# Four of eight gate/up K-steps as three single-pass products, one buffer for the down parts, and a new order on ScalarE and VectorE

## The chip, the core and the metric

One core of a Trainium2 chip. The metric is the device time of one execution in microseconds (us), the median of several. TensorE does matrix products and transposes, ScalarE (ACT) copies and activations, VectorE (DVE) elementwise work, GpSimd (POOL) here issues the indexed gathers and scatters, SyncE (SP) issues the plain loads and stores. The engines run side by side and wait for each other on semaphores.

## The reference, cut to what matters

A diffusion backbone step over 256 context and 1024 latent tokens (1280 rows of 1024). A mixing layer is followed by a mixture of 16 experts, of which each token takes two; both carry float32 data.

```python
gate = jnp.einsum('btd,edf->btef', h, w_eg)      # d = 1024, f = 256, 16 experts
up = jnp.einsum('btd,edf->btef', h, w_eu)
a = jax.nn.silu(gate) * up * combine.astype(h.dtype)[..., None]   # combine: 2 experts of 16 per token
return jnp.einsum('btef,efd->btd', a, w_ed)
```

The result, scaled by a gate row, is added to the residual, and a last RMS norm follows. The change touches the expert part only.

## The kernel before, in words

The kernel first runs the modulation, projection, Fourier, convolution and mLSTM parts, then the output projection and router (to about 800 us of the span). The router's result sorts the 2560 (token, expert) pairs by expert into slots of 128 rows; each slot has one expert. The inputs give 27 slots, numbered 0 to 26 here. All numbers of slots, the expert of a slot (`eidI`), the place of its weights (`offI`) and each expert's last slot (`endI`) are read from tables at run time by register loads.

*Weights.* An expert takes `WE` = 6144 columns of float32 in each of 128 partitions: 4096 for gate and up (8 K-steps of 512 columns) and 2048 for down. Three experts fit in `wexp`, a ring. SP loads an expert in three pieces of 1 MB (line 645). The load of expert e + 3 waits until the last slot of expert e has been through `down` (`dn_ps`, line 663), and until all earlier loads have landed (`w_full`).

*One slot.* POOL gathers its 128 rows of `h2` from memory into `xg` (`fetch`, line 772). TensorE transposes them (`x_trans`, line 1580) into two PSUM banks; ScalarE copies them out (`x_chan`, lines 1137 and 1138). `gate_up` accumulates 8 K-steps of 128 x 512 in one bank, silu comes from ScalarE (`gate_silu`, line 1166), the product with up from VectorE (`product`, line 2188). `a_trans` (line 1602) transposes the result, `down` multiplies it into 1024 columns (two banks), `out_rows` on VectorE computes the gate row (`gate_rows`, line 2216) and scales the rows (`scaled_rows`, line 2223), and POOL adds them to `acc_scratch` in memory by an indexed scatter (`add_rows`, line 791). A scatter waits for the one before (`added`); the gather for a later slot is behind it in POOL's queue.

*Products in parts.* Most products are plain float32 (two records in the trace for one K-step). Others are split: an operand is copied to a type called fp32r, the high part, and what is left over is a second fp32r operand, the low part. Three single-pass products, high x high, low x high and high x low, then take the place of one float32 product. Before the change `SK` = 2 of the 8 gate/up K-steps and all of down are done in parts. High parts are ScalarE copies (`gate_high` line 1151, `down_high` line 1161, `a_high` line 1142, the second copy of `x_chan`); low parts are VectorE subtractions (`gate_low` line 2203, `down_low` line 2211, `a_low` line 2192, `x_low` line 2197). `esplit` holds the parts of gate/up and down of two slots.

*Order.* TensorE's loop has in step n: `a_trans` of slot n, `x_trans` of slot n + 2, `gate_up` of slot n + 1, `down` of slot n. ScalarE's in step n: `a_high` (n), `x_chan` (n + 2), `down_high` (n + 1), `gate_silu` (n + 1), `gate_high` (n + 2). VectorE's: `a_low` (n), `x_low` (n + 2), `down_low` (n + 1), `product` (n + 1), `out_rows` (n), `gate_low` (n + 2). The orders are written out by hand. `gate_high` and `down_high` load two registers each, then wait for the weights of their slot. In the last steps VectorE also makes two one-hot rows (`slot_owner`, line 2264), since the last two slots' rows are added on TensorE instead of by a scatter; SP loads the sums for the final norm after the second of these. Ahead of the loop VectorE runs `slot_weights` and `slot_weights_in`; the latter waits for products of TensorE (`per_slot`) that come after `gate_up` of slot 0.

## Time and profile before

| | us |
|---|---|
| median of 3 runs | 1139.44 |
| lowest, highest | 1138.89, 1149.29 |
| the profiled execution | 1137.51 |
| its span | 1135.7 |
| TensorE busy in the span | 1045.4 (92%) |
| VectorE busy | 668.5 (59%) |
| ScalarE busy | 417.9 (37%) |

The profiler records one execution. The span runs from its first to its last instruction; all times in rows below are us from its start unless marked ns. In a timeline row stand the start, the time, the engine (PE is TensorE's matmuls, PEld its weight loads, SPq and POOLq the queues that issue DMAs), the line of the kernel, the operation, its output and inputs and how many instructions were merged; in square brackets the idle time of the engine before it and what ended it.

### The profile page before, as it was taken

The page shows a single profiled execution, that of the slowest core. Times are in us where ns is not written, and L with a number is a line of the kernel's source. Part 1 is how long each engine was busy: PE and PEld are TensorE (multiplying, and loading weights), DVE is VectorE, ACT ScalarE, POOL GpSimd, SP SyncE. Part 2 cuts the span into 40 slices and gives each one's busy share as a digit, 9 for nine tenths or more (in the row PEclk, how much of TensorE's full clock was granted, in tenths as well). Part 3 has the DMA queues.
Part 4 walks back from the last instruction along what each step waited for, and adds up shares of the span by engine and source line. Part 5 has one row for each costly group of instructions (what it writes and reads, how often), then busy time and mean ns, then how long its engine had stood idle before and what let it go on. Part 6 is the DMA issues. An engine that isn't in the chain of part 4 may idle for free.

```text
span 1135.7 us, 18439 instructions
## 1 busy us (share of the span) xinstructions
PE 1045.4 (92%) x6090; PEld 789.5 (70%) x6091; DVE 668.5 (59%) x1137; ACT 417.9 (37%) x816; POOL 200.0 (18%) x240
## 2 busy tenths in 40 slices
PE   6899999999999999989877999992699999989997
PEld 3899999989999986569764444541456666656665
DVE  3445885177798410119994443366666666666677
ACT  3443223244322246246662111121244445444444
POOL 2010000000000002002355000000233433333413
PEclk9899999999999998999998999996799999999999
DMA  9934333314342231322136222225748889887957
GB/s 370 343 126 147 118 140 131 111 57 148 111 142 102 94 135 47 93 87 64 54 50 241 111 90 97 93 93 203 278 124 276 274 250 280 268 301 228 320 147 291
DMA packets 59303, 188.36 MB, mean 166 GB/s; under 512 B 8018, under 2 KB 20818, under 8 KB 53106
## 3 DMA queue, kind: packets, MB, share of 16 engines
q1 hardware_dynamic: 49924, 154.81, 38.0%
q0 software_dynamic: 7632, 27.79, 10.2%
q10 hardware_dynamic: 1696, 5.10, 1.1%
q8 instruction: 29, 0.48, 0.2%
q14 instruction: 22, 0.18, 0.0%
HBM read 153.52 MB, written 34.16 MB: 165 GB/s over the span
## 4 chain that ended last, share of the span: by engine, by line
PE 80%; DVE 9%; DMA 3%; issue 2%; ACT 2%; POOL 1%; SPq 1%; POOLq 0%; ACTq 0%; DVEq 0%
PE psum L1345 43%; PE psum L1287 29%; DVE RW L1922 3%; PE psum L1580 2%; DVE RE L1949 1%; PE psum L1211 1%; DMA RB<-in_w_exp 1%; DMA RA<-in_w_ada 1%; DVE RE L1957 1%; PE psum L1500 1%; PE psum L1302 1%; DMA RW<-h_scratch,idxc 1%; PE psum L1227 1%; PE psum L1266 1%; PE psum L1602 0%
## 5 line engine op out<-in xcount | busy, mean ns | idle before, releaser
L1287 PE MATMUL psum<-input_parts,weight_parts 128*128 128x320 f32 x2208 | 339.3, 313 | 1.7 <-DVE input_parts L1721 1.7
L1287 PEld LDWEIGHTS psum<-input_parts,weight_parts 128*128 128x128 f32 x2208 | 325.7, 189 | 10.4 <-issue 6.9
L1345 PE MATMUL psum<-RB,RW 128*128 x324 | 148.0, 607 | 6.1 <-DMA RB<-in_w_exp 3.5
L921 ACT ACTIVATE weight_parts<-RW 128x1024 fp32r<-128x1024 f32 x46 | 48.7, 1058 | 224.7 <-PE psum L1287 224.7
L1345 PE MATMUL psum<-expert_parts 128*128 128x512 f32 x486 | 126.5, 413 | 1.1 <-DVE expert_parts L2192 1.1
L1728 DVE TENSOR_TENSOR weight_parts<-RW,weight_parts 128x1024 fp32r<-128x1024 f32 x46 | 56.3, 1225 | 113.4 <-ACT weight_parts L921 113.2
L1345 PEld LDWEIGHTS psum<-expert_parts 128*128 128x128 f32 x486 | 91.3, 188 | 31.7 <-issue 13.5
L1345 PEld LDWEIGHTS psum<-RB,RW 128*128 128x128 f32 x324 | 60.8, 195 | 74.7 <-issue 74.6
L1345 PE MATMUL psum<-RS,RB 128*128 128x512 f32 (+1 forms) x200 | 80.1, 555 | 1.4 <-DVE RE L1949 1.2
L1345 PE MATMUL psum<-RC,RB 128*128 128x512 f32 x160 | 74.8, 613 | 0.0
L732 POOL TENSOR_TENSOR RE<-RE,RA 2x2304 f32<-2x2304 f32 (+1 forms) x2 | 9.0, 4520 | 348.6 <-DMA RA<-in_b_ada 348.5
L2211 DVE TENSOR_TENSOR expert_parts<-RB,expert_parts 128x1024 fp32r<-128x1024 f32 x54 | 63.7, 1222 | 9.8 <-ACT expert_parts L1161 9.0
L1345 PEld LDWEIGHTS psum<-RS,RB 128*128 128x128 f32 x200 | 37.1, 190 | 38.1 <-issue 35.0
L1740 DVE SCALAR_TENSOR_TENSOR RB<-RB,colv 128x15 f32<-128x15 f32 x120 | 57.3, 552 | 0.0
L1161 ACT ACTIVATE expert_parts<-RB 128x1024 fp32r x54 | 54.1, 1049 | 6.5 <-issue 5.8
L1345 PEld LDWEIGHTS psum<-RC,RB 128*128 128x128 f32 x160 | 30.0, 197 | 31.1 <-issue 31.1
L1151 ACT ACTIVATE expert_parts<-RB 128x1024 fp32r x27 | 28.6, 1061 | 61.4 <-DMA RB<-in_w_exp 38.7
L2223 DVE SCALAR_TENSOR_TENSOR RE<-psum,maskf,RC 128x1024 f32<-128x1024 f32 x27 | 34.6, 1283 | 23.7 <-PE psum L1345 21.8
L2066 DVE TENSOR_TENSOR RA<-psum,RB 128x1024 f32<-128x1024 f32 x10 | 12.2, 1224 | 57.3 <-PE psum L1345 57.1
L791 POOL DMA_INDIRECT acc_scratch<-RE,idxsc x25 | 44.0, 1758 | 7.2 <-issue 7.1
L1166 ACT ACTIVATE RB<-psum 128x256 f32<-128x256 f32 x27 | 10.3, 383 | 92.2 <-PE psum L1345 92.2
L2188 DVE TENSOR_TENSOR RB<-RB,psum 128x256 f32<-128x256 f32 x27 | 11.4, 421 | 54.8 <-ACT RB L1166 54.6
(351 smaller groups left out, 1522.7 us busy)
## 6 DMA issues: line engine op xcount, KB each, us to landing
RB<-in_w_exp SPq DMA_DIRECT2D x48, 1024.0 KB, 8.9
RW<-in_w_in SPq DMA_DIRECT2D x46, 512.0 KB, 4.1
RW<-in_w_ada SPq DMA_DIRECT2D x34, 512.0 KB, 3.3
RA<-in_w_ada SPq DMA_DIRECT2D x10, 512.0 KB, 14.1
RW<-gm_scratch SPq DMA_DIRECT2D x20, 256.0 KB, 3.4
h_scratch<-RE SPq DMA_DIRECT2D x10, 512.0 KB, 2.6
acc_scratch<-RA SPq DMA_DIRECT2D x10, 512.0 KB, 3.6
RB<-acc_scratch SPq DMA_DIRECT2D x10, 512.0 KB, 8.6
```

What stands on the lines that cost most here:

```text
L791: nc.gpsimd.indirect_dma_start(acc_dram, bass.IndirectOffsetOnAxis(ap=idxsc[:, r], axis=0), yb[:, r], None, compute_op=ALU.add).then_inc(a ...
L921: nc.scalar.activation(spl[:, r, 0], raw[:, r], ACT.Copy).then_inc(whi_ok, 1)
L1151: nc.scalar.activation(esplit[:, r, 0, 0:G_U], wexp[:, bass.ds(off, G_U)], ACT.Copy).then_inc(whi_ok, 1)
L1161: nc.scalar.activation(esplit[:, r, 0, G_U + j * D:G_U + (j + 1) * D], wexp[:, bass.ds(off + (D_U + j * D), D)], ACT.Copy)\
L1287: last = nc.tensor.matmul(psum[:, 2 * r + g, 0:GW], spl[:, r, wv, k], hT[:, xv, k, g * GW:(g + 1) * GW], start=(k == 0 and wv == 0 and xv ...
L1345: return nc.tensor.matmul(out, lhsT, rhs, start=start, stop=stop, **kw_)
L1580: last = nc.tensor.transpose(psum[:, 4 + k // 4, (k % 4) * P:(k % 4 + 1) * P], xg[:, r, k * P:(k + 1) * P], ident[:, :])
L1728: nc.vector.tensor_tensor(spl[:, r, 1], raw[:, r], spl[:, r, 0].bitcast(F32), ALU.subtract).then_inc(wlo_ok, 1)
L1740: nc.vector.scalar_tensor_tensor(out, u[:, bass.ds(i, n)], colv[:, bass.ds(i * 2 + (C_WDW + j), 1)], out, ALU.mult, ALU.add).then_inc(conv, 1)
L1922: nc.vector.scalar_tensor_tensor(Dm[:, n % 2, hd], nmb[:, n % 2, hd], gcol[:, 0, t, d, hd:hd + 1], (maskf if d == 0 else maskb)[:, :], ALU ...
L2211: nc.vector.tensor_tensor(esplit[:, r, 1, c], wexp[:, bass.ds(off + (D_U + j * D), D)], esplit[:, r, 0, c], ALU.subtract)\
L2223: nc.vector.scalar_tensor_tensor(yb[:, r].rearrange("p (b c) -> p b c", b=2), psum[:, bank:bank + 2, :], wslot[:, col], gates.rearrange("p ...
```

## The change

`SK` goes from 2 to 4: four gate/up K-steps are float32, four are in parts. The low part of x moves to a place in `RW` that the smaller `xT` frees. `esplit` is replaced by `gsplit` (gate/up parts of two slots, 2048 columns each) and one `dsplit` for the down parts of one slot; the last slot's down parts go to the gate/up buffer `lsplit` that is free by then. `gate_high` and `gate_low` have two instructions each. `down_high` and `down_low` work on slot n in step n, not n + 1. The order becomes, on ScalarE in step n: `a_high` (n), `down_high` (n), `x_chan` (n + 2), `gate_high` (n + 2), `gate_silu` (n + 1); on VectorE: `a_low` (n), `down_low` (n), `x_low` (n + 2), `gate_low` (n + 2), `product` (n + 1), `out_rows` (n). TensorE's order stays.

```diff
-SK = 2
+SK = 4
...
     with nc.sbuf_tensor("expert_parts", [P, 8 * T + 4 * D], F32R) as expert_parts:
-        esplit = expert_parts[:, 0:12 * D].rearrange("p (b v n) -> p b v n", b=2, v=2)
+        gsplit = expert_parts[:, 0:8 * D].rearrange("p (b v n) -> p b v n", b=2, v=2)
+        dsplit = expert_parts[:, 8 * D:12 * D].rearrange("p (v n) -> p v n", v=2)
+        lsplit = gsplit[:, 1]
         aTh, aTl = (expert_parts[:, c:c + 2 * FE].rearrange("p (b j t) -> p b j t", b=2, j=2) for c in (12 * D, 12 * D + 2 * FE))
...
@@ -1148,17 +1153,17 @@
             if read is not None:
                 act.wait_ge(gu_ps, read)
             act.wait_ge(x1_out, 16 * (NT - BATCH))
-            nc.scalar.activation(esplit[:, r, 0, 0:G_U], wexp[:, bass.ds(off, G_U)], ACT.Copy).then_inc(whi_ok, 1)
-
-        def down_high(r, blk, read):
+            for q in range(2):
+                nc.scalar.activation(gsplit[:, r, 0, q * D:(q + 1) * D], wexp[:, bass.ds(off + q * D, D)], ACT.Copy).then_inc(whi_ok, 1)
+
+        def down_high(dst, blk, done, read):
             need = act.value_load(eidI[0:1, blk], min_val=16 * WPART, max_val=16 * WPART * NE)
             off = act.value_load(offI[0:1, blk], min_val=0, max_val=2 * WE)
             act.wait_ge(w_full, need)
-            if read is not None:
-                act.wait_ge(dn_ps, read)
+            act.wait_ge(done, read)
             act.wait_ge(x1_out, 16 * (NT - BATCH))
             for j in range(2):
-                nc.scalar.activation(esplit[:, r, 0, G_U + j * D:G_U + (j + 1) * D], wexp[:, bass.ds(off + (D_U + j * D), D)], ACT.Copy)\
+                nc.scalar.activation(dst[:, 0, j * D:(j + 1) * D], wexp[:, bass.ds(off + (D_U + j * D), D)], ACT.Copy)\
                     .then_inc(whi_ok, 1)
...
         gate_high(0, slice(0, 1), None)
         x_chan(0, 1)
-        down_high(0, slice(0, 1), None)
+        gate_high(1, slice(1, 2), None)
         gate_silu(0, 1)
         x_chan(1, 2)
-        act.wait_ge(tok_ps, 2)
-        gate_high(1, slice(1, 2), None)
+
+        def step(j, n):
+            a_high(j, n + 1)
+            down_high(dsplit, bass.ds(n, 1), dn_ps, n + 1)
+            x_chan(j, n + 3)
+            gate_high(j, bass.ds(n + 2, 1), n + 1)
+            gate_silu(1 - j, n + 2)
+
         with act.Fori(0, pairs) as i:
             for j in range(2):
-                r = 1 - j
-
-                a_high(j, i * 2 + (1 + j))
-                x_chan(j, i * 2 + (3 + j))
-                down_high(r, bass.ds(i * 2 + (1 + j), 1), i * 2 + (1 + j))
-                gate_silu(r, i * 2 + (2 + j))
-                gate_high(j, bass.ds(i * 2 + (2 + j), 1), i * 2 + (1 + j))
+                step(j, i * 2 + j)
+        step(0, pairs * 2)
         n = pairs * 2 + 1
-        a_high(0, n)
-        x_chan(0, n + 2)
-        down_high(1, bass.ds(n, 1), n)
-        gate_silu(1, n + 1)
-        gate_high(0, bass.ds(n + 1, 1), n)
         a_high(1, n + 1)
+        down_high(dsplit, bass.ds(n, 1), dn_ps, n + 1)
         x_chan(1, n + 3)
-        down_high(0, bass.ds(n + 1, 1), n + 1)
+        down_high(lsplit, bass.ds(n + 1, 1), gu_ps, n + 1)
         gate_silu(0, n + 2)
         a_high(0, n + 2)
...
             for k in range(SK, KD):
-                mm(psum[:, r, :], xT[:, r, k], wexp[:, bass.ds(off + k * 2 * FE, 2 * FE)], k == SK, False)
+                mm(psum[:, r, :], xT[:, r, k - SK], wexp[:, bass.ds(off + k * 2 * FE, 2 * FE)], k == SK, False)
             pe.wait_ge(xl_ok, have)
             pe.wait_ge(wlo_ok, split)
             for k in range(SK):
                 for xp, v in ((xTh, 0), (xTl, 0), (xTh, 1)):
-                    last = mm(psum[:, r, :], xp[:, r, k], esplit[:, r, v, k * 2 * FE:(k + 1) * 2 * FE], False,
+                    last = mm(psum[:, r, :], xp[:, r, k], gsplit[:, r, v, k * 2 * FE:(k + 1) * 2 * FE], False,
                               k == SK - 1 and v == 1)
             last.then_inc(gu_ps, 1)
...
-        gate_up(0, slice(0, 1), 1, SPLIT0 + 1)
+        gate_up(0, slice(0, 1), 1, SPLIT0 + 2)
         per_slot(blkw, 3, 3, 4)
         x_trans(1, 16, 1)
         with pe.Fori(0, pairs) as i:
             for j in range(2):
                 a_trans(j, i * 2 + (1 + j))
                 x_trans(j, i * 16 + 32, i * 2 + (2 + j))
-                gate_up(1 - j, bass.ds(i * 2 + (1 + j), 1), i * 2 + (2 + j), i * 6 + (SPLIT0 + 4 + 3 * j))
-                down(j, i * 2 + (1 + j), i * 6 + (SPLIT0 + 3 + 3 * j))
+                gate_up(1 - j, bass.ds(i * 2 + (1 + j), 1), i * 2 + (2 + j), i * 8 + (SPLIT0 + 4 + 4 * j))
+                down(j, i * 2 + (1 + j), i * 8 + (SPLIT0 + 6 + 4 * j), dsplit)
         a_trans(0, pairs * 2 + 1)
-        down(0, pairs * 2 + 1, pairs * 6 + (SPLIT0 + 3), 0)
+        down(0, pairs * 2 + 1, pairs * 8 + (SPLIT0 + 4), lsplit, 0)
...
         def gate_low(r, blk, split):
             off = dve.value_load(offI[0:1, blk], min_val=0, max_val=2 * WE)
-            dve.wait_ge(whi_ok, split)
-            nc.vector.tensor_tensor(esplit[:, r, 1, 0:G_U], wexp[:, bass.ds(off, G_U)], esplit[:, r, 0, 0:G_U], ALU.subtract)\
-                .then_inc(wlo_ok, 1)
-
-        def down_low(r, blk, split):
+            for q in range(2):
+                dve.wait_ge(whi_ok, split + q)
+                c = slice(q * D, (q + 1) * D)
+                nc.vector.tensor_tensor(gsplit[:, r, 1, c], wexp[:, bass.ds(off + q * D, D)], gsplit[:, r, 0, c], ALU.subtract)\
+                    .then_inc(wlo_ok, 1)
+
+        def down_low(dst, blk, split):
             off = dve.value_load(offI[0:1, blk], min_val=0, max_val=2 * WE)
             for j in range(2):
                 dve.wait_ge(whi_ok, split + j)
-                c = slice(G_U + j * D, G_U + (j + 1) * D)
-                nc.vector.tensor_tensor(esplit[:, r, 1, c], wexp[:, bass.ds(off + (D_U + j * D), D)], esplit[:, r, 0, c], ALU.subtract)\
+                c = slice(j * D, (j + 1) * D)
+                nc.vector.tensor_tensor(dst[:, 1, c], wexp[:, bass.ds(off + (D_U + j * D), D)], dst[:, 0, c], ALU.subtract)\
                     .then_inc(wlo_ok, 1)
...
         x_low(0, 1)
         slot_weights()
-        down_low(0, slice(0, 1), SPLIT0 + 2)
         slot_weights_in()
+        gate_low(1, slice(1, 2), SPLIT0 + 3)
         product(0, 1)
         x_low(1, 2)
-        gate_low(1, slice(1, 2), SPLIT0 + 4)
+
+        def step(j, n):
+            at = lambda k: slice(n + k, n + k + 1) if isinstance(n, int) else bass.ds(n + k, 1)
+            a_low(j, n + 1)
+            down_low(dsplit, at(0), n * 4 + (SPLIT0 + 5))
+            x_low(j, n + 3)
+            gate_low(j, at(2), n * 4 + (SPLIT0 + 7))
+            product(1 - j, n + 2)
+            out_rows(j, n, at(0))
+
         for j in range(2):
-            a_low(j, 1 + j)
-            x_low(j, 3 + j)
-            down_low(1 - j, slice(1 + j, 2 + j), SPLIT0 + 5 + 3 * j)
-            product(1 - j, 2 + j)
-            out_rows(j, j, slice(j, j + 1))
-            gate_low(j, slice(2 + j, 3 + j), SPLIT0 + 7 + 3 * j)
+            step(j, j)
         with dve.Fori(0, pairs) as i:
             for j in range(2):
-                a_low(j, i * 2 + (3 + j))
-                x_low(j, i * 2 + (5 + j))
-                down_low(1 - j, bass.ds(i * 2 + (3 + j), 1), i * 6 + (SPLIT0 + 11 + 3 * j))
-                product(1 - j, i * 2 + (4 + j))
-                out_rows(j, i * 2 + (2 + j), bass.ds(i * 2 + (2 + j), 1))
-                gate_low(j, bass.ds(i * 2 + (4 + j), 1), i * 6 + (SPLIT0 + 13 + 3 * j))
+                step(j, i * 2 + (2 + j))
         n = pairs * 2 + 2
-        a_low(0, n + 1)
-        x_low(0, n + 3)
-        down_low(1, bass.ds(n + 1, 1), pairs * 6 + (SPLIT0 + 11))
-        product(1, n + 2)
-        out_rows(0, n, bass.ds(n, 1))
-        gate_low(0, bass.ds(n + 2, 1), pairs * 6 + (SPLIT0 + 13))
+        step(0, n)
         a_low(1, n + 2)
-        down_low(0, bass.ds(n + 2, 1), pairs * 6 + (SPLIT0 + 14))
+        down_low(dsplit, bass.ds(n + 1, 1), pairs * 8 + (SPLIT0 + 17))
+        down_low(lsplit, bass.ds(n + 2, 1), pairs * 8 + (SPLIT0 + 19))
         def slot_owner(b):
             c = n + (3 + b - LATE)
             nc.vector.tensor_scalar(owner[:, b], token, rowid[:, bass.ds(c, 1)], None, ALU.is_equal).then_inc(onehot, 1)
```

## Rows read from the trace of the kernel before

**Rows 1.** The page's part 4: shares of the chain that ended last, by line.

```profile
PE psum L1345 43%; PE psum L1287 29%; DVE RW L1922 3%; PE psum L1580 2%; DVE RE L1949 1%; PE psum L1211 1%; DMA RB<-in_w_exp 1%; DMA RA<-in_w_ada 1%; DVE RE L1957 1%; PE psum L1500 1%; PE psum L1302 1%; DMA RW<-h_scratch,idxc 1%; PE psum L1227 1%; PE psum L1266 1%; PE psum L1602 0%
```

**Rows 2.** Windows, one loop step; PE, PEld, DVE, ACT, POOL busy, clock, DMA share, GB/s.

```profile
888.24:898.60 10.36, 10.36 (x42) 6.71 (x41) 7.05 (x8) 4.86 (x8) 4.79 (x4) 1.00 0.87 304
```

**Rows 3.** Timeline of the same step, TensorE's weight loads.

```profile
888.24 0.37 PEld L1602 LDWEIGHTS psum<-ident,RB 128*128 128x128 f32 x2
...
890.42 0.19 PEld L1345 LDWEIGHTS psum<-RB,RW 128*128 128x128 f32 x1 [0.24 <-issue]
...
894.28 0.19 PEld L1345 LDWEIGHTS psum<-expert_parts 128*128 128x128 f32 x1 [0.24 <-issue]
...
894.71 3.84 PEld L1345 LDWEIGHTS psum<-expert_parts 128*128 128x128 f32 x17 [0.24 <-issue]
...
898.59 0.37 PEld L1602 LDWEIGHTS psum<-ident,RB 128*128 128x128 f32 x2
```

**Rows 4.** Timeline of the same step, ScalarE and VectorE.

```profile
888.88 0.38 ACT L1142 ACTIVATE expert_parts<-psum 128x256 fp32r<-128x256 f32 x1 [0.49 <-PE psum L1602]
...
888.93 1.28 DVE L2223 SCALAR_TENSOR_TENSOR RE<-psum,maskf,RC 128x1024 f32<-128x1024 f32 x1 [0.96 <-PE psum L1345]
...
889.76 0.81 ACT L1137 ACTIVATE RW<-psum 128x768 f32<-128x768 f32 x1 [0.49 <-PE psum L1580]
...
891.17 2.00 ACT L1161 ACTIVATE expert_parts<-RB 128x1024 fp32r x2 [0.33 <-issue]
...
892.37 2.36 DVE L2211 TENSOR_TENSOR expert_parts<-RB,expert_parts 128x1024 fp32r<-128x1024 f32 x2 [0.37 <-ACT expert_parts L1161]
...
896.29 0.38 ACT L1166 ACTIVATE RB<-psum 128x256 f32<-128x256 f32 x1 [3.12 <-PE psum L1345]
...
897.75 1.06 ACT L1151 ACTIVATE expert_parts<-RB 128x1024 fp32r x1 [1.08 <-issue]
```

**Rows 5.** Timelines of SP and ScalarE around 1000 us, and a window as in rows 2.

```profile
993.14 1.58 SPq L645 DMA_DIRECT2D RB<-in_w_exp  x3
...
1000.58 0.38 ACT L1166 ACTIVATE RB<-psum 128x256 f32<-128x256 f32 x1 [3.12 <-PE psum L1345]
...
1007.85 1.06 ACT L1151 ACTIVATE expert_parts<-RB 128x1024 fp32r x1 [6.89 <-DMA RB<-in_w_exp]
...
1004.00:1008.00 4.00, 0.48 (x5) 0.25 (x4) 0.87 (x1) 0.15 (x1) 0.57 (x2) 1.00 0.75 246
```

**Rows 6.** Line 645, the loads that go out from 919 to 922 us.

```profile
L645 SPq DMA_DIRECT2D RB<-in_w_exp x3: 332/333/333, 919.9 to 921.0; - x3
...
DMA to landing us min/median/max: 6.5/10.0/13.9
```

**Rows 7.** Timeline and a window at the start of the expert loop.

```profile
821.39 0.41 DVE L2188 TENSOR_TENSOR RB<-RB,psum 128x256 f32<-128x256 f32 x1
...
825.16 7.11 PE L1345 MATMUL psum<-RB,RW 128*128 x12 [0.70 <-issue]
...
826.00:828.00 2.00, 2.00 (x4) 0.95 (x3) 0.92 (x2) 1.93 (x2) 0.67 (x2) 0.50 0.05 18
```

**Rows 8.** Timeline at the end of the expert loop.

```profile
1096.02 0.88 DVE L2264 TENSOR_SCALAR row_of_slot<-RC,maskf 128x1280 fp32r<-128x1280 f32 x1
...
1098.23 0.42 DVE L2188 TENSOR_TENSOR RB<-RB,psum 128x256 f32<-128x256 f32 x1
...
1101.84 2.59 PEld L1345 LDWEIGHTS psum<-expert_parts 128*128 128x128 f32 x12 [1.35 <-issue]
```

**Rows 9.** POOL's waits (us, times, longest); a gather, its landing, and the transposes reading it.

```profile
POOL idxsc L790 <- DMA acc_scratch<-RE,idxsc: 88.3, 15, 8.5
...
957.72 1.01 POOL L772 DMA_INDIRECT RW<-h_scratch,idxc  x1 [0.16 <-issue]
...
DMA to landing us min/median/max: 11.9/11.9/11.9
...
971.68 1.04 PE L1580 MATMUL psum<-ident,RW 128*128 128x128 f32 x8
```

More of the change, by code:

```diff
@@ L230, in program @@
     xg = RW[:, 0:2 * D].rearrange("p (b c) -> p b c", b=2)
-    xT = RW[:, 2 * D:4 * D].rearrange("p (b k t) -> p b k t", b=2, k=KD)
+    xT = RW[:, 2 * D:3 * D].rearrange("p (b k t) -> p b k t", b=2, k=KD - SK)
     mb = 3 * WE
@@ L242, in program @@
     rowid = maskf[:, 2 * NBLK:3 * NBLK]
-    yparts = expert_parts[:, 6 * D:12 * D].rearrange("p (v n) -> p v n", v=2)[:, :, D:D + LATE * D].rearrange("p v (b c) -> p v b c", b=LATE)
+    yparts = dsplit.rearrange("p v (b c) -> p v b c", b=LATE)
     SUM_BANK = (4, 6, 2, 0)
@@ L1603, in a_trans, with down @@
             last.then_inc(at_ps, 1)
-        def down(r, n, split, bank=2):
+        def down(r, n, split, parts, bank=2):
             pe.wait_ge(ah_ok, n)
@@ L1612, in down @@
                 for j in range(2):
-                    c = G_U + j * D + g * 512
+                    c = j * D + g * 512
                     for ap, v in ((aTh, 0), (aTl, 0), (aTh, 1)):
-                        last = mm(psum[:, bank + g, :], ap[:, r, j], esplit[:, r, v, c:c + 512], j == 0 and ap is aTh and v == 0,
+                        last = mm(psum[:, bank + g, :], ap[:, r, j], parts[:, v, c:c + 512], j == 0 and ap is aTh and v == 0,
                                   j == 1 and v == 1)
```

7 lines of the change are left out of this document (5 added, 2 removed).

## Prediction, made before the change was run

> **What bounds the kernel now.** I read the chain that ended last first: the matmul helper on line 1345 carries 43% of the span [rows 1], and from 825 us to 1100 us nearly all of it is the expert loop. Then the windows: in one loop step of 10.36 us TensorE is busy for all of it, VectorE for 7.05, ScalarE for 4.86, the DMA engines for 0.87 of it [rows 2]. So TensorE sets the pace and only its own time or a new wait counts. Then the timeline of one step, with time counted from its start, the first weight load of `a_trans`, at 888.24 [rows 3].
>
> TensorE: transposes 1.2; six full-precision K-steps as twelve instructions (x12 in [rows 7]), nine of which start over 890.42 to 894.28, 0.429 each; then 6 + 12 single-pass products, seventeen weight loads in 3.84, so (3.84 - 0.19)/16 = 0.228 each [rows 3]. The next step starts at 10.35.
>
> The others [rows 4]: `scaled_rows` at 0.69, `a_high` at 0.64, `x_chan` at 1.52, `down_high` at 2.93 (two pieces in 2.00), `down_low` 0.14 after the first piece has ended (two in 2.36), `gate_silu` at 8.05, `gate_high` at 9.51. Between the start of an instruction and the next one that needs two register loads lie about 1.4 us (889.76 to 891.17; 896.29 to 897.75). I use that 1.4 below.
>
> **The change, part by part.** Times are against the profiled execution, 1137.51 (span 1135.7).
>
> *Products.* Each slot loses 2 K-steps, 4 x 0.429 = 1.716, and gains 6 x 0.228 = 1.368: 0.35 less, a step of 10.0 instead of 10.35. Over 27 slots: **-9.4**. No more can be had, since nothing else is taken from TensorE.
>
> *ScalarE and VectorE work in a steady step.* Added: one 1024-column copy (1.06 on ScalarE, row of 897.75) and one 1024-column subtraction (1.18 on VectorE) [rows 4]; `x_low` doubles to 512 columns, a size the trace does not show. It lies between 0.41 for 256 columns [rows 7] and 1.22 for 1024; I take 0.68. `x_chan` still copies 1024 columns, split 512 and 512 rather than 768 and 256: nothing. I place the new order in a step. ScalarE: `a_high` 0.64; `down_high` 0.64 + 1.4 = 2.04 to 4.04; `x_chan` to 5.14; `gate_high` 4.04 + 1.4 = 5.44 to 7.44; `gate_silu` at 8.05 - 0.35 = 7.70. VectorE: `scaled_rows` 0.69 to 1.97, `a_low` to 2.31, `down_low` 3.24 to 5.60, `x_low` to 6.20, `gate_low` 6.64 to 9.00, product to 9.34, `gate_rows` to 10.54, `scaled_rows` at 10.0 + 0.69 = 10.69. Dues: `down` starts at 7.1 and needs 5.60; `a_trans` at 10.0 needs 9.34. So TensorE stays the pace, with 0.66 to spare on product and 0.15 on `gate_rows`: the cost is 0, and if the cover goes, every us beyond these is paid in each of some 24 steps. Queued behind a late `gate_low` are the product and through it `a_trans`.
>
> *One buffer for the down parts.* `down_high` now waits for the `down` of the slot before. That one ends ahead of `a_trans`, and `a_high`, ahead of `down_high` on ScalarE, needs `a_trans`: 0. Below nothing is excluded, since before it TensorE never waited for down parts in a steady step.
>
> *`gate_high` is moved ahead of `gate_silu`.* It waits for the weights of the slot after next; `gate_silu`, the product and `a_trans` of the next slot are now queued behind that wait. Before, the silu had already gone. From a landing at w, second copy w + 2.06, subtractions w + 3.6, product w + 4.0; so w later than 5.95 in the step is a TensorE stall. Before, the same wait came at 9.5 with nothing urgent behind it. One expert is late beyond doubt: its first load instruction goes out at 993.14, in a step that began at 1000.58 - 8.05 = 992.53, and its copy starts at 1007.85, w = 15.3 [rows 5]. Before, this cost TensorE 3.5 us (0.48 busy of 4.00). Now `a_trans` waits until 15.3 + 4.05 = 19.3 rather than 10.0: 9.3. Net, with 0.2 for what the old idle ended late, **+5.6**. Bounds: nothing if the weights came 9 us sooner (nothing in the change makes them), 6.6 if they come one us later.
>
> *The clock after it.* TensorE stood idle for 3.5 us there and kept a granted clock of 1.00 (2.4 GHz) [rows 5]; after the broken-up stretch before 825 us it had 0.50 (1.2 GHz) for about 4 us [rows 7]. An idle stretch of 9 us has no row here in the loop. I take it as the second case: 4 us at half rate lose **+2.0**; bounds 0 and 3.9 (the whole first product group at half rate). The Trainium skill, "TensorE: Matmul & The Clock Gate", section "Why this matters for your kernels", says that an idle gap between bursts puts TensorE back on the lower level; by that rule too the loss is there, and without it the sum would be 2.0 lower. The 3.5 us row stayed at full clock, so the trace does not bear the rule out at that length.
>
> *Other experts.* The load that goes out from 919.91 on lands at 921.0 + 13.9 = 934.9 [rows 6]. Its step began 0.6 before that, as with the late one, at 919.3, so w is 15.6 one step earlier; less one new step of 10.0 that is 5.6 against 5.95: 0.35 to spare, where before it had 4 us. Two more (slots 14 and 17) stand at 0.4 and 0.7 by the same reckoning. The rows gather and scatter chain on POOL is tight as well: it waited 88.3 us in 15 waits for its own last scatter [rows 9], and the gather issued at 957.72 landed 11.9 later, at 969.6, 2 us ahead of the transposes that read it (971.68); eight steps of 0.35 less since the chain last waited for VectorE take 2.8 of which the chain had slack for 2. I take **+1.0** for all of these; bounds 0 and 6 (four at 1.5).
>
> *Start.* `gate_low` of slot 1, 2.36, is now ahead of product(0), which ran at 821.39 [rows 7]; before it came behind. So product(0) ends at 823.8 rather than 821.8, `x_low` at 824.4, transposes follow, and `gate_up` of slot 1 starts near 826.25 rather than 825.16: +1.1, beside the 0.35 that slot 0 had gained: **+1.5**. Bounds 0.5 (value loads of 0.70 hidden) and 2.5.
>
> *Tail.* VectorE builds two sets of down parts, a one-hot row of 0.88 and `gate_rows` before the last product: 9.00 + 0.80 + 1.19 = 10.9 in the step, where it ran at 8.47, as in the middle (8.05 for the silu and 0.42), so that this step began at 1098.23 - 8.47 = 1089.76. After it come the second one-hot, `gate_rows` and `a_low`, and the last `down` (1101.84, that is 12.1 in the step) starts at 13.9 instead of 11.7 [rows 8]: **+2.2**. Bounds 1 and 3. The loads of the final sums, behind the second one-hot on SP, move by the same amount and stay in step.
>
> Sum: -9.4 + 5.6 + 2.0 + 1.0 + 1.5 + 2.2 = +2.9: 1140.4 for an execution like the profiled one. The median shown is 1.9 above it (1139.44), so by median **1142.3**, 0.25% more: no change. 1% of this kernel, about what a measurement tells from nothing, is 11.4 us.
>
> **The rivals.**
> 1. *Only the products count*: the late expert costs no more than before because its load goes out earlier or contention falls, the clock stays, the edges hide. -9.4 plus 0 to 4: about 1133 by median. For it: 0.66 of cover in the steady step. Against: ScalarE's queue is strictly in order and w = 15.3 is a measured landing.
> 2. *VectorE's round becomes the pace (slower)*. Place: product behind two `gate_low`. It decides from 0.66 us of added delay a step. The gaps before `down_high` and `gate_high` are estimates from two places; if each is 0.5 longer, the product ends at 10.34 and the step is 10.4, as before. Then the 9.4 is gone while the rest stays: 1137.5 + 12.3 + 1.9 = 1151.7. For it: VectorE has 8.5 of 10.0 busy by my sum (7.05 + 1.18 + 0.27). Against: the chain has slack by measured pieces.
> 3. *Transfers become the pace*: at 0.87 share in a step [rows 2], a step 3% shorter makes each of the tight landings 2 us late: +5 more, 1147. For it rows 6 and 9; against: each stall gives the queues time back.
>
> **How the numbers follow.** Forecast 0.60, rival 1 0.15, rival 2 0.13, rival 3 0.12. Low end: forecast less the clock, the +1.0 and part of the edges, 1134; high end takes in rival 3 and most of rival 2: 1153. Faster by over 1% would need under 1128.0, below even -9.4 (1130.0): 0.03. Slower by over 1% needs over 1150.8: rival 2 and the upper tail of rival 3, 0.15. Within: 0.82.
>
> **What would show it.** Steady steps of 10.0 with TensorE busy throughout (wrong if 10.3 or more: rival 2, with idle before line 1602 released by VectorE's product). One idle of 9 us before the `a_trans` of slot 17 released through ScalarE by the expert load, and half clock behind it. Short waits of `gate_high` for weights at slots 12, 14, 17. First product near 823.4. Idle of 1 to 2 us before the last `a_trans`. Were the step 10.0 and no 9 us idle seen, the moved wait was my error.

## The result, and the profile after

| | before | after |
|---|---|---|
| median of 20 runs each | 1140.43 us | 1148.19 us |
| lowest, highest | 1132.37, 1149.29 | 1141.31, 1156.52 |
| the profiled execution, its span | 1137.51, 1135.7 | 1150.82, 1147.7 |

The ratio is 1.0069, 95% interval 1.0047 to 1.009: 7.9 us slower, under 1%. The page of after, its part 1 and the shares of the chain by engine and by line:

```profile
PE 1045.0 (91%) x6144; PEld 805.0 (70%) x6145; DVE 705.1 (61%) x1164; ACT 438.2 (38%) x843; POOL 210.2 (18%) x240
...
PE 64%; DMA 14%; DVE 9%; issue 6%; ACT 3%; POOL 2%; SPq 1%; POOLq 0%; ACTq 0%; DVEq 0%
...
PE psum L1289 29%; PE psum L1347 29%; DMA acc_scratch<-RE,idxsc 8%; DMA RW<-h_scratch,idxc 3%; DVE RW L1924 2%; DVE RE L1951 1%; PE psum L1213 1%; DMA RB<-in_w_exp 1%; DMA RA<-in_w_ada 1%; PE psum L1502 1%; DVE RE L1959 1%; PE psum L1582 1%; PE psum L1304 1%; PE psum L1229 1%; PE psum L1268 1%
```

TensorE's busy time is the same as before, although its products became shorter. The part ahead of the expert loop, which the change does not touch, was busy for 2.0 us more in this execution. From the first gather on TensorE is busy for 310.4 us where it was 312.9. The shorter products alone would save 6.5 there (25 steps of 0.26, from the table below), but products at half clock take some 4 more (2.2 behind slot 18, 1.6 at the end, both below). In the chain DMA has 14%. More than half of it are the scatters into `acc_scratch`, which [rows 1] does not list at all: transfers now appear where TensorE had been. TensorE itself still did not wait for them in most of these steps, so the shares alone do not say what the time went to.

A steady loop step of after, from its timeline; its first weight load of `a_trans` was at 1036.99, one step before the last row:

```profile
1038.74 0.19 PEld L1347 LDWEIGHTS psum<-RB,RW 128*128 128x128 f32 x1 [0.24 <-issue]
...
1041.32 0.19 PEld L1347 LDWEIGHTS psum<-expert_parts 128*128 128x128 f32 x1 [0.24 <-issue]
...
1039.04 2.00 ACT L1166 ACTIVATE expert_parts<-RB 128x1024 fp32r x2 [1.02 <-issue]
...
1040.24 2.36 DVE L2215 TENSOR_TENSOR expert_parts<-RB,expert_parts 128x1024 fp32r<-128x1024 f32 x2 [0.95 <-ACT expert_parts L1166]
...
1041.91 2.00 ACT L1157 ACTIVATE expert_parts<-RB 128x1024 fp32r x2
...
1042.52 0.69 DVE L2199 TENSOR_TENSOR x_parts<-psum,expert_parts 128x512 fp32r<-128x512 f32 x1
...
1043.12 2.35 DVE L2207 TENSOR_TENSOR expert_parts<-RB,expert_parts 128x1024 fp32r<-128x1024 f32 x2
...
1044.74 0.38 ACT L1171 ACTIVATE RB<-psum 128x256 f32<-128x256 f32 x1 [0.83 <-PE psum L1347]
...
1045.39 0.42 DVE L2190 TENSOR_TENSOR RB<-RB,psum 128x256 f32<-128x256 f32 x1
...
1047.04 0.37 PEld L1604 LDWEIGHTS psum<-ident,RB 128*128 128x128 f32 x2
```

These answer to [rows 3, 4]. The step takes 10.05. The single-pass part begins at 1041.32, 1.7 us earlier in the step than before. `down_high` starts at 2.05, `down_low` at 3.25, the two `gate_low` at 6.13, product at 8.40: the layout in the prediction, which had 2.04, 3.24, 6.64 and 9.00. The `x_low` of 512 columns took 0.69. VectorE is busy 8.47 in ten us, TensorE all of it (this window has the columns of [rows 2]):

```profile
843.00:853.00 10.00, 10.00 (x43) 7.01 (x42) 8.47 (x9) 5.54 (x9) 4.17 (x5) 1.00 0.66 144
```

Then slot 18, whose expert comes late (timelines of SP, ScalarE and TensorE, and a window):

```profile
995.54 1.53 SPq L650 DMA_DIRECT2D RB<-in_w_exp  x3
...
992.59 0.38 ACT L1171 ACTIVATE RB<-psum 128x256 f32<-128x256 f32 x1 [1.51 <-PE psum L1347]
...
1010.40 2.00 ACT L1157 ACTIVATE expert_parts<-RB 128x1024 fp32r x2 [10.44 <-DMA RB<-in_w_exp]
...
1012.31 0.36 ACT L1171 ACTIVATE RB<-psum 128x256 f32<-128x256 f32 x1
...
1014.34 0.69 PE L1604 MATMUL psum<-ident,RB 128*128 128x128 f32 x2 [8.94 <-DVE RB L2190]
```

```profile
1014.00:1016.00 2.00, 1.66 (x8) 1.66 (x9) 1.81 (x3) 0.38 (x1) 0.00 (x0) 0.50 1.01 426
```

`gate_high` waits 10.44 us for the load sent from 995.54 on. Behind it the silu, for which the matmuls had long been done, goes at 1012.31, and TensorE stands for 8.94 us, where it stood for 3.5 in [rows 5]. The window behind shows clock 0.50 at 1.66 us busy of 2.00.

Both edges. First, at the start, `gate_low` of slot 1, the product behind it and the transposes that wait for it; then, at the end, product, `a_trans` and the last `down` of slot 26, and a window there:

```profile
824.84 2.36 DVE L2207 TENSOR_TENSOR expert_parts<-RB,expert_parts 128x1024 fp32r<-128x1024 f32 x2 [0.56 <-issue]
...
827.12 0.42 DVE L2190 TENSOR_TENSOR RB<-RB,psum 128x256 f32<-128x256 f32 x1
...
827.59 0.44 PE L1604 MATMUL psum<-ident,RB 128*128 128x128 f32 x2 [3.17 <-DVE RB L2190]
```

```profile
1108.81 0.41 DVE L2190 TENSOR_TENSOR RB<-RB,psum 128x256 f32<-128x256 f32 x1
...
1109.28 0.44 PE L1604 MATMUL psum<-ident,RB 128*128 128x128 f32 x2 [0.41 <-DVE RB L2190]
...
1112.03 4.59 PE L1347 MATMUL psum<-expert_parts 128*128 128x512 f32 x12 [2.31 <-DVE expert_parts L2194]
```

```profile
1112.00:1114.00 2.00, 1.97 (x5) 1.59 (x6) 0.98 (x1) 0.98 (x1) 0.00 (x0) 0.50 1.01 401
```

The last twelve products take 4.59 rather than 3.00, at clock 0.50, after 2.31 idle. The same products in the kernel before:

```profile
1101.84 3.00 PE L1345 MATMUL psum<-expert_parts 128*128 128x512 f32 x12 [1.12 <-DVE expert_parts L2192]
```

**A table for all kernels.** The parts ahead of the expert loop are the same in every kernel here, yet the first gather started anywhere between 798.05 and 809.94 us. So I compare from that gather on, and cut the rest at the starts of the silus (one a slot, 0 to 26), read from each timeline of ScalarE:

| kernel | gather to silu 0 | 0 to 1 | 1 to 16 | 16 to 18 | 18 to 26 | 26 to end | sum |
|---|---|---|---|---|---|---|---|
| before | 19.8 | 13.8 | 156.5 | 24.5 | 83.1 | 37.9 | 335.6 |
| after | 19.1 | 15.0 | 155.0 | 32.0 | 81.6 | 41.5 | 344.3 |
| old_gate_first | 19.8 | 13.9 | 156.7 | 31.9 | 83.1 | 37.8 | 343.2 |
| new_silu_first | 19.2 | 15.0 | 159.9 | 21.1 | 83.1 | 41.9 | 340.2 |
| old_light_loads | 19.1 | 12.2 | 155.3 | 20.7 | 82.8 | 37.9 | 328.0 |
| new_light_loads | 19.3 | 15.1 | 151.6 | 20.2 | 80.7 | 42.2 | 329.0 |
| new_edges | 18.8 | 13.7 | 154.7 | 33.2 | 81.6 | 40.3 | 342.2 |
| new_early_loads | 20.5 | 17.0 | 152.0 | 20.3 | 80.9 | 41.0 | 331.7 |
| new_silu_first_gather | 19.5 | 14.9 | 152.7 | 27.5 | 81.6 | 41.7 | 337.8 |
| new_all_mended | 19.4 | 13.8 | 152.7 | 21.0 | 81.7 | 40.3 | 328.9 |
| old_mended_transfers | 18.8 | 13.8 | 158.2 | 20.9 | 84.8 | 37.6 | 334.1 |
| new_all_silu_first | 19.3 | 13.8 | 152.6 | 20.2 | 81.4 | 39.3 | 326.6 |

After against before, 8.7 us in one pair of profiles: the stretch at slot 18 +7.5, the end +3.6, the start +0.6, the other steps -1.5 and -1.5.

Each row of the table is one execution, while the ratios below come from 9 to 12 of each kernel against the kernel before in the same rounds. The two can differ by several us: new_edges is 6.6 us above before in the table and 1.5 by its ratio; new_silu_first_gather is 2.2 above in the table and 3.3 below by its ratio (its profiled execution, 1149.87, was the slowest of its twelve). So the table is used for where time went, and the ratios for how much.

### The profile page after: what moved, and what is told of

It reads as the page before. It is cut to its first block, busy times and chain, and to the rows that moved or that the text cites. A ratio compares the mean times of both kernels' runs of the same rounds, so it can differ in the third digit from the quotient of the medians.

```text
span 1147.7 us, 18640 instructions
## 1 busy us (share of the span) xinstructions
PE 1045.0 (91%) x6144; PEld 805.0 (70%) x6145; DVE 705.1 (61%) x1164; ACT 438.2 (38%) x843; POOL 210.2 (18%) x240
## 3 DMA queue, kind: packets, MB, share of 16 engines
q0 software_dynamic: 7632, 27.79, 10.2%
## 4 chain that ended last, share of the span: by engine, by line
PE 64%; DMA 14%; DVE 9%; issue 6%; ACT 3%; POOL 2%; SPq 1%; POOLq 0%; ACTq 0%; DVEq 0%
PE psum L1289 29%; PE psum L1347 29%; DMA acc_scratch<-RE,idxsc 8%; DMA RW<-h_scratch,idxc 3%; DVE RW L1924 2%; DVE RE L1951 1%; PE psum L1213 1%; DMA RB<-in_w_exp 1%; DMA RA<-in_w_ada 1%; PE psum L1502 1%; DVE RE L1959 1%; PE psum L1582 1%; PE psum L1304 1%; PE psum L1229 1%; PE psum L1268 1%
## 5 line engine op out<-in xcount | busy, mean ns | idle before, releaser
L1347 PE MATMUL psum<-expert_parts 128*128 128x512 f32 x540 | 159.2, 417 | 2.3 <-DVE expert_parts L2194 2.3
L1347 PEld LDWEIGHTS psum<-expert_parts 128*128 128x128 f32 x540 | 102.6, 190 | 31.5 <-issue 7.8
L1347 PE MATMUL psum<-RB,RW 128*128 x216 | 103.0, 622 | 5.1 <-issue 2.7
L2215 DVE TENSOR_TENSOR expert_parts<-RB,expert_parts 128x1024 fp32r<-128x1024 f32 x54 | 63.8, 1222 | 27.8 <-ACT expert_parts L1166 27.8
L1347 PEld LDWEIGHTS psum<-RB,RW 128*128 128x128 f32 x216 | 41.0, 200 | 49.0 <-issue 48.8
L2207 DVE TENSOR_TENSOR expert_parts<-RB,expert_parts 128x1024 fp32r<-128x1024 f32 x54 | 63.6, 1219 | 16.5 <-ACT expert_parts L1157 15.1
L1157 ACT ACTIVATE expert_parts<-RB 128x1024 fp32r x54 | 54.1, 1056 | 37.4 <-issue 25.5
L1166 ACT ACTIVATE expert_parts<-RB 128x1024 fp32r x54 | 54.1, 1049 | 30.4 <-issue 25.1
L796 POOL DMA_INDIRECT acc_scratch<-RE,idxsc x25 | 50.7, 2030 | 9.3 <-issue 9.3
L2068 DVE TENSOR_TENSOR RA<-psum,RB 128x1024 f32<-128x1024 f32 x10 | 12.2, 1225 | 56.8 <-PE psum L1347 56.6
L1347 PE MATMUL psum<-RC,RW 128*128 128x129 f32 x320 | 42.3, 289 | 1.0 <-DVE RE L1959 1.0
```

Source lines behind the costliest of these rows:

```text
L796: nc.gpsimd.indirect_dma_start(acc_dram, bass.IndirectOffsetOnAxis(ap=idxsc[:, r], axis=0), yb[:, r], None, compute_op=ALU.add).then_inc(a ...
L1157: nc.scalar.activation(gsplit[:, r, 0, q * D:(q + 1) * D], wexp[:, bass.ds(off + q * D, D)], ACT.Copy).then_inc(whi_ok, 1)
L1166: nc.scalar.activation(dst[:, 0, j * D:(j + 1) * D], wexp[:, bass.ds(off + (D_U + j * D), D)], ACT.Copy)\
L1347: return nc.tensor.matmul(out, lhsT, rhs, start=start, stop=stop, **kw_)
L2207: nc.vector.tensor_tensor(gsplit[:, r, 1, c], wexp[:, bass.ds(off + q * D, D)], gsplit[:, r, 0, c], ALU.subtract)\
L2215: nc.vector.tensor_tensor(dst[:, 1, c], wexp[:, bass.ds(off + (D_U + j * D), D)], dst[:, 0, c], ALU.subtract)\
```

## Experiments

Theory M: `gate_high`, moved ahead of the silu, puts a late load in TensorE's path. Rival V: VectorE's added work. Rival D: the shorter step presses the transfers.

### The moved wait alone, in the kernel before

In every step, and at the edges of the loop:

```diff
-                gate_silu(r, i * 2 + (2 + j))
                 gate_high(j, bass.ds(i * 2 + (2 + j), 1), i * 2 + (1 + j))
+                gate_silu(r, i * 2 + (2 + j))
...
-                product(1 - j, i * 2 + (4 + j))
-                out_rows(j, i * 2 + (2 + j), bass.ds(i * 2 + (2 + j), 1))
                 gate_low(j, bass.ds(i * 2 + (4 + j), 1), i * 6 + (SPLIT0 + 13 + 3 * j))
+                product(1 - j, i * 2 + (4 + j))
+                out_rows(j, i * 2 + (2 + j), bass.ds(i * 2 + (2 + j), 1))
```

> The kernel before with one move: gate_high ahead of gate_silu on ScalarE, gate_low ahead of product on VectorE; products and buffers as before. Theory M (the moved wait): one idle of TensorE of about 9 us ahead of the a_trans of slot 17 in place of 3.5, released through VectorE's product by ScalarE and the late expert load, half clock for some 4 us behind it: +7 us against the kernel before (ratio 1.006). Rival V (VectorE's added work is what costs): nothing is added here, so no difference, ratio 1.000, and at most 4 us idle. Rival D (the shorter step presses the transfers): the step is unchanged at 10.35, so also 1.000.

Measured: 1.004 (1.0007 to 1.0073), where 1.006 was expected: 4.3 us by the medians of the same rounds. In the table only 16 to 18 differs from before by more than 0.2, and by 7.4 us. ScalarE's and TensorE's rows there:

```profile
1011.41 1.06 ACT L1151 ACTIVATE expert_parts<-RB 128x1024 fp32r x1 [12.12 <-DMA RB<-in_w_exp]
...
1014.21 0.69 PE L1602 MATMUL psum<-ident,RB 128*128 128x128 f32 x2 [8.84 <-DVE RB L2188]
```

The order alone, with nothing added to VectorE and the step as long as before, makes the idle of 8.84. Theory M stands for this part, and V and D cannot explain it.

### The change with the old place of the silu

```diff
-            gate_high(j, bass.ds(n + 2, 1), n + 1)
             gate_silu(1 - j, n + 2)
+            gate_high(j, bass.ds(n + 2, 1), n + 1)
...
-            gate_low(j, at(2), n * 4 + (SPLIT0 + 7))
             product(1 - j, n + 2)
             out_rows(j, n, at(0))
+            gate_low(j, at(2), n * 4 + (SPLIT0 + 7))
```

> The kernel after with gate_silu put back ahead of gate_high, and product and out_rows ahead of gate_low; four K-steps in parts stay. Theory M: the 9 us idle falls to about 4 and the half clock behind it goes: 7 us less than the kernel after, so about level with the kernel before (1.000, 0.997 to 1.003). The step may grow from 10.05 to 10.2, since gate_low now ends 4.3 into the next step and pushes down_low to 7.1, just when down wants it. Rival V: no better than after, 1.007 or more. Rival D: the idle stays, since the load is as late as before.

Measured: 1.0031 (0.9998 to 1.0063), half of what was hoped for, and its interval still touches 1. 16 to 18 fell from 32.0 to 21.1, below even before. But TensorE stood elsewhere (TensorE's timeline and a window):

```profile
981.33 1.94 PE L1582 MATMUL psum<-ident,RW 128*128 128x128 f32 x8 [4.00 <-DMA RW<-h_scratch,idxc]
...
983.94 5.28 PE L1347 MATMUL psum<-RB,RW 128*128 x8 [0.67 <-issue]
```

```profile
984.00:986.00 2.00, 2.00 (x3) 0.97 (x4) 0.69 (x1) 0.39 (x1) 0.93 (x2) 0.50 0.83 246
```

The transposes wait 4.00 for a gather, and half clock follows: a step of 17.7. That is rival D, beside M. The load of slot 18 was late by hardly anything (0.6 idle); a run below, without this stall, has 5.0 idle there, so the stall had given the load its time. Two transfers compete to be the late one.

### Light loads, new and old

```diff
-                sp.dma_start(wexp[:, r * WE + q * WP:r * WE + (q + 1) * WP], src[:, q * WP:(q + 1) * WP]).then_inc(w_full, 16)
+                sp.dma_start(wexp[:, r * WE + q * WP:r * WE + q * WP + WP // 4], src[:, q * WP:q * WP + WP // 4]).then_inc(w_full, 16)
```

> The kernel after with each expert load cut to the first 512 of its 2048 columns per piece (the products use what the buffers held there, so the output is of no use). No load is then late. Theory M: no idle near slot 17, and against the kernel after some 11 us less (8.9 idle and 2 of clock), against the kernel before about 0.997 of its time. Rival V: the step is bound by VectorE and stays, 1.004 or more. Rival D: steps get shorter and more even, the tight ones with 10.3 to 10.6 fall to 10.05.

> The kernel before with the same cut of the loads (output of no use). Its only cost from them was the 3.5 us wait, so 3 to 4 us less than before, ratio 0.997. The pair with new_light_loads shows the change without late weights: by theory M 27 x 0.35 less on products, plus 1.5 at the start and 2 to 3.5 at the end, so the pair differs by 4 to 6 us in favour of the new; by rival V by nothing or against it.

Measured: new 0.9916 (0.9883 to 0.9948), old 0.9916 (0.9886 to 0.9946). The new gained against after, 1148.19 to 1132.2, more than the 11 expected. All its steps are 10.04 to 10.24, so V is out: with its full work on VectorE the step is TensorE's. The old gained more than the 3.5 expected, too: its uneven steps became 10.35 to 10.36, and the start 1.7 faster. And the pair is level, where 4 to 6 us in favour of the new were expected. The table says why: silu 1 to 26 is 6.4 us shorter in the new (25 steps of 0.26), its start 3.1 longer and its end 4.3. So the edges alone eat the products' gain, before any load is late. More than half of that is TensorE's clock. At the start the old kernel's twelve products of slot 1 took 5.41, where they took 7.11 in [rows 7]; at the end the new kernel's last `down` took 5.48, where it took 3.00 in before:

```profile
828.78 5.41 PE L1345 MATMUL psum<-RB,RW 128*128 x12 [0.71 <-issue]
```

```profile
1094.55 5.48 PE L1347 MATMUL psum<-expert_parts 128*128 128x512 f32 x12 [2.31 <-DVE expert_parts L2194]
```

### The two edges mended

```diff
         slot_weights_in()
-        gate_low(1, slice(1, 2), SPLIT0 + 3)
         product(0, 1)
         x_low(1, 2)
+        gate_low(1, slice(1, 2), SPLIT0 + 3)
...
-        down_low(lsplit, bass.ds(n + 2, 1), pairs * 8 + (SPLIT0 + 19))
...
         slot_owner(0)
         gate_rows(n + 1, bass.ds(n + 1, 1), gmix, n + 2)
         product(0, n + 3)
+        down_low(lsplit, bass.ds(n + 2, 1), pairs * 8 + (SPLIT0 + 19))
         slot_owner(1)
         dve.wait_ge(onehot, 4 + LATE)
-        gate_rows(n + 2, bass.ds(n + 2, 1), gmix_last, n + 2)
         a_low(0, n + 3)
         scaled_rows(1, n + 1, bass.ds(n + 1, 1), 2, gmix)
+        gate_rows(n + 2, bass.ds(n + 2, 1), gmix_last, n + 2)
```

> The kernel after with VectorE's order changed at the two edges alone: product of slot 0 and x_low ahead of gate_low of slot 1; at the end product of slot 26 ahead of the second set of down parts. The loop is untouched. If the edges cost what the traces of before and after show (slot 0's silu to slot 1's: 14.99 against 13.84; slot 26's silu to the end: 41.5 against 37.9), 1.1 and 2 to 3.5 us come back: from the first gather to the end 340.5 to 341.5, where it was 344.3, ratio to before 1.003. Rival: the half clock seen in the last down product (4.6 us for twelve, before 3.0) has nothing to do with the late product and stays; then only 2.5 in all come back.

Measured: 1.0013 (0.9984 to 1.0041). The start came back in full (13.7). Of the end only 1.2 did, and the last products still ran at half clock:

```profile
1108.99 4.59 PE L1347 MATMUL psum<-expert_parts 128*128 128x512 f32 x12 [2.16 <-DVE expert_parts L2194]
```

The rival written down for this run was right: the half clock stays although the product is no longer late. It does not belong to this place as such, though. Of the full kernels with the change only new_all_silu_first got below 40.0 at the end (39.3), and there the same products ran at clock 1.00, behind an idle no shorter:

```profile
1094.24 3.01 PE L1350 MATMUL psum<-expert_parts 128*128 128x512 f32 x12 [2.27 <-DVE expert_parts L2198]
```

### Loads of the gate/up columns sent earlier

The first two pieces of a load need only that `gate_up` is done with the place, which the silu of the expert's last slot shows. `sg_ok` gets one more count at the start, like `dn_ps`, so that the table's number fits, and `product` waits for one more.

```diff
             for q in range(WPART):
+                if q == 2 and done is not None:
+                    sp.wait_ge(dn_ps, done)
                 sp.dma_start(...)
...
-                sp.wait_ge(dn_ps, done)
-                load_expert(r, src, None)
+                sp.wait_ge(sg_ok, done)
+                load_expert(r, src, None, done)
```

> The kernel after, but the first two pieces of an expert's load (the gate/up columns) wait for the silu of the last slot that used the place, not for its down; the third piece still waits for down. Orders of ScalarE and VectorE are those of the change. Theory M: the load for slot 18 goes out some 13 us sooner, ahead of its need, so the 9 us idle and the half clock behind it go: 10 us or so less than the kernel after, ratio to before 0.997 to 1.000. Rival V: idle gone, time of a step up, little gained. Rival D: with the stall gone the gathers fall behind, since the chain of scatters on POOL takes 10.6 us a slot in that stretch against 10.05: an idle of 2 to 6 us before a transpose, released by a gather, eats half of it.

Measured: 0.9958 (0.9924 to 0.9992), against 1.0069 of the change as it is: 1.1% for moving one wait on SP. The loads and `gate_high` of slot 18:

```profile
988.11 12.71 SPq L652 DMA_DIRECT2D RB<-in_w_exp  x3
...
1005.49 2.01 ACT L1159 ACTIVATE expert_parts<-RB 128x1024 fp32r x2 [0.53 <-DMA RB<-in_w_exp]
```

The first pieces go at 988.1, 180.0 after the first gather and not 192.1 as in after; the wait is 0.53, 16 to 18 is 20.3, and the other steps are 10.05 to 10.55. The idle that rival D foretold did not come, so a short step alone does not make the gathers late. Whether the loads' earlier start or the order of VectorE kept them in time here was not separated. The start took 17.0, two more than after. TensorE's idle there is the same (3.16 for 3.17); the eight float32 products of slot 1 took 6.70 where they took 4.69 in after, more of them at half clock.

### Gathers ahead of scatters

On POOL, in new_silu_first; the loop's indices move by one:

```diff
         for j in range(2):
             refill(1, j)
-            add_rows(j, j, slice(j + 1, j + 2))
+        add_rows(0, 0, slice(1, 2))
         with gp.Fori(0, pairs) as i:
             for j in range(2):
                 refill(i + 2, j)
-                add_rows(j, i * 2 + (2 + j), bass.ds(i * 2 + (3 + j), 1))
+                add_rows(1 - j, i * 2 + (1 + j), bass.ds(i * 2 + (2 + j), 1))
+        add_rows(1, pairs * 2 + 1, bass.ds(pairs * 2 + 2, 1))
```

> new_silu_first, and on POOL each gather issued one scatter earlier (ahead of it instead of behind). new_silu_first had its old place of gate_high but an idle of 4.0 us before the transposes of one step, released by a gather, and a silu-to-silu time of 17.7 there. Theory D (gathers queued behind the scatter chain): that idle and its half clock go, and about 3.5 us of idle come up at slot 18 instead, as the expert's load is late again: 3 to 5 us less than new_silu_first. Rival: the gather is late because of the traffic and not of its place in the queue: the idle stays at 3 us or more.

Measured: 0.9971 (0.9943 to 0.9998). No gather is waited for any more, and the load of slot 18 is late again, for the `gate_up` as in the kernel before:

```profile
1016.19 5.39 PE L1348 MATMUL psum<-RB,RW 128*128 x8 [5.02 <-DMA RB<-in_w_exp]
```

The mechanism went as expected, with 5.0 of idle rather than 3.5, and half clock behind it (a step of 17.0). Against new_silu_first it is 0.6% by the ratios, within the 3 to 5 us expected, and 2.4 us in the table.

### All of it, and the control

> The change with its own loop order, and all three remedies: both edges, earlier loads of gate/up columns, gathers ahead of scatters. If theory M, the edges and D are the whole of it, steps are 10.05 throughout with no idle over 1 us in the loop: from the first gather to the end 26 steps of 10.07, about 327 to 330, ratio to before 0.990 to 0.995, below both kernels. If VectorE's load matters (V), steps of 10.3 and more are left without any transfer being late, and the ratio is 1.000.

> The kernel before (two K-steps in parts, old orders) with the same two remedies for the transfers: earlier loads of the gate/up columns and gathers ahead of scatters. It tells what of new_all_mended is the change's and what the remedies'. By theory M and the product sum the old step stays at 10.35 without idle at slot 18: from the first gather to the end 335.6 less 3.8 less some 0.8 of uneven steps, 331; ratio to before 0.996. new_all_mended had 328.9, so the change would be worth 2 us once its transfers and edges are mended. Rival: the old kernel does no better than before (its 3.5 us come back elsewhere), ratio 1.000.

> new_all_mended with gate_silu ahead of gate_high and product ahead of gate_low. If late loads are no longer there, the order should not matter for them, and steps are bound by TensorE either way: within 2 us of new_all_mended, ratio to before 0.990 to 0.995. If the product's small spare time under the change's order cost something (steps of 10.3 to 11.1 after a slow register load), this one is 1 to 2 us faster.

The edits are those above: new_all_mended has edges, early loads and gathers; old_mended_transfers has early loads and gathers in the kernel before; new_all_silu_first adds the old place of the silu to the first. Measured: 0.9921 (0.989 to 0.9952), 0.995 (0.9924 to 0.9975), 0.9921 (0.9888 to 0.9954). The first and the third beat both kernels: 1132.29 and 1132.14 us median against 1140.43 and 1148.19. Of their 0.8% the remedies give 0.5% without the change, and what is left for the change, 0.3%, lies within intervals that overlap. Two of the three ran in the same rounds on one chip, so they can be compared directly: new_all_silu_first has a mean of 1132.4 (10 runs), old_mended_transfers 1136.7 (12 runs). The difference of 4.2 us has a 95% interval of 0.8 to 7.7, worked out from the single runs. That is a first sign that four K-steps in parts are worth something with their edges and transfers mended; it was not repeated. The order of silu and `gate_high` no longer matters to the time.

Not all of it went as expected. new_all_mended still has two steps of 11.0 and 11.1, where 10.05 throughout was expected. In old_mended_transfers the stall of slot 18 is gone, but the other steps became less even (158.2 and 84.8 us for 156.5 and 83.1), so that it came to 334.1 in the table and not 331.

## Why the prediction was right in kind and short in size

The time (1148.2 forecast as 1142.3) lies in the range, and TensorE's step, the late expert, the clock behind it and the late products at both edges were as placed. The sum was +2.9 against the profiled execution and came to +7.9 by medians. Nothing cancelled: the three terms that were off (products, tail, transfers) all erred towards too fast. The range held because it was wide enough, not because each term was right. Its low end, 1134, also lies above rival 1's own 1133. Term by term:

- *Products, -9.4.* Over-sized. A step of 10.05 to 10.10 instead of 10.0; between light kernels 0.26 a step, some -6.8 over 26 steps. The single-pass products are a little slower than assumed: with six of them in place of two float32 K-steps, the weight loads of after stand 0.70 apart for three, 0.233 each (0.228 was read off a run of down and gate/up together):

```profile
885.38 0.42 PEld L1347 LDWEIGHTS psum<-expert_parts 128*128 128x128 f32 x2
...
886.08 0.42 PEld L1347 LDWEIGHTS psum<-expert_parts 128*128 128x128 f32 x2
```

- *One buffer, the doubled `x_low`, the added copies, 0.* Right. The copy and the subtraction lie beside TensorE's work.
- *Late expert +5.6 and clock +2.0.* Right: 8.94 idle against 3.52 is +5.4, and the next step took 12.3 for 10.05, +2.2. old_gate_first shows both without the rest.
- *Start +1.5.* Right: +1.2 from silu 0 to silu 1 and the 0.35 lost in it.
- *Tail +2.2.* The term that failed: +3.6 from the last silu to the end. The late start of the last `down` was there (5.84 after the silu, before 4.02; 1.8 where 2.2 was forecast). The half clock behind its idle, 1.6 more (4.59 for 3.00), was not in the sum: the prediction priced the clock for the long idle alone. How much of it is paid differs from kernel to kernel: nothing in new_all_silu_first, 2.5 in new_light_loads. The idle of 1 to 2 us that was to show before the last `a_trans` was 0.41; the rest of the wait came behind it, before `down`.
- *Tight transfers +1.0.* Under-sized: silu 1 to 16 should have been 3.9 shorter at 0.26 a step and was 1.5, and 18 to 26 was 1.5 for 2.1: 3 us in all. A typical uneven step:

```profile
883.70 2.01 ACT L1166 ACTIVATE expert_parts<-RB 128x1024 fp32r x2 [2.27 <-issue]
...
890.04 0.41 DVE L2190 TENSOR_TENSOR RB<-RB,psum 128x256 f32<-128x256 f32 x1
...
892.99 2.41 PE L1347 MATMUL psum<-RB,RW 128*128 x5 [1.02 <-issue]
```

ScalarE was idle for 2.27 us by "issue" (register loads) ahead of `down_high` instead of 1.0, so the chain of copies and subtractions ended late, with the product at 890.04. That used up its slack and cost nothing: `a_trans` began at 890.71, 10.09 after the one before. What made the next step long (11.34) is TensorE's own gap of 1.02 "issue" between `x_trans` and `gate_up`, where TensorE loads two registers. Counted from `a_trans` to `a_trans`, seven steps of after between silu 1 and silu 26, beside the two at slot 18, are over 10.2; in six of them this stretch is what is longer, by 4.2 us in all. The kernel before has four such steps (10.5 to 10.9), by the same stretch and 1.5 us in all; one of them:

```profile
879.10 5.41 PE L1345 MATMUL psum<-RB,RW 128*128 x12 [0.22 <-issue]
```

So the difference, 2.7 of the 3 us, is more and longer gaps of a kind that was there before. Where loads are light they are gone in the old kernel and 0.2 at most in the new. That they come from the traffic fits this; what in the register loads or the fetch of instructions is slowed was not tried.

Together: -6.8 + 5.4 + 2.2 + 1.5 + 3.6 + 3.0 = +8.9 less 0.6 ahead of silu 0, near the 8.7 between the profiles.

Rival 2 (VectorE as the pace) is refuted by the even 10.04 to 10.24 of new_light_loads. Rival 3 was real but elsewhere than placed. `gate_high` did wait shortly for weights at slots 12 and 17, as foretold (0.71 and 0.73; not at 14), but TensorE did not stand for either. It stood for the gathers, and in the change as it is they cost 0.39 us at one place only. The wait at slot 17:

```profile
989.07 2.01 ACT L1157 ACTIVATE expert_parts<-RB 128x1024 fp32r x2 [0.73 <-DMA RB<-in_w_exp]
```

Rival 1 fell with the idle of 8.94.

## What to carry to other kernels

When a hand-written order is changed on an engine that runs its queue in order, ask of each wait what stands behind it and not only what it waits for: moving a wait for a late transfer ahead of an instruction on the path cost 7.4 us here between two profiles (4.3 by medians) with no work added. Look at the slack of transfers in steps, not at the mean share of the DMA engines; a load sent when its place is really free gave 1.1%. And price the edges of a loop, TensorE's clock behind their idles included: of 27 slots' gain of 6 to 7 us, start and end took 4 with full loads and 7 with light ones.
